# Scaling the token rows before the transpose, in place of a product with a diagonal, at three layer entrances

## The chip, the cores and the metric

The kernel runs on one core of one Trainium2 chip. The metric is the device time of one execution, in microseconds. Engines are named as in the profile: PE is TensorE (PEld its weight loads), DVE is VectorE, ACT is ScalarE, POOL is GpSimd, SP the engine that issues the weight DMAs.

## The reference, cut to what matters

Four mixers and two MLPs are applied in turn to 256 tokens of width 1024, all in f32. Each of them starts from a root-mean-square norm:

```python
def rms_norm(x, g):
    xf = x.astype(jnp.float32)
    y = xf * lax.rsqrt(jnp.mean(xf * xf, axis=-1, keepdims=True) + NORM_EPS)
    return (y * g.astype(jnp.float32)).astype(x.dtype)

def adaln_pre_norm(x, c, g, w_mod, b_mod):
    mod = jax.nn.silu(c) @ w_mod + b_mod
    shift, scale, gate = jnp.split(mod, 3, axis=-1)
    h = rms_norm_2(x, g, NORM_EPS) * (1.0 + scale[:, None, :]) + shift[:, None, :]
    return h, gate
```

The order is: sparse attention (dsa), MLP 0, the RWKV mixer, MLP 1, a norm in the middle, a short convolution mixer (conv), a dilated attention mixer (dil), a last norm. The three entrances of this case are those of the RWKV mixer (plain `rms_norm`), of conv and of dil (both `adaln_pre_norm`).

## The kernel before, in words

The activations `X` lie with the tokens on the partitions, as two tiles of 128 tokens by 1024. Each linear layer wants them with the features on the partitions, in eight blocks of 128. Weights come as granules of 128x1024 into a ring of four slots: SP's DMA fills `raw`, ACT rounds it to `w_hi` (L737), DVE takes the rest `w_lo` (L1350, `split_lo`), and PE makes three products per tile (hi·hi, hi·lo, lo·hi). The activations are split in the same way into `act_hi` (ACT) and `act_lo` (DVE). Each engine has its own program, written out by hand in a fixed order, and semaphores join them. SP may load granule g once `w_lo` of granule g-4 is made, and ACT may round it once PE is done with granule g-4.

An entrance goes as follows, for token tile i = 0 and then 1. ACT sums the squares of `X` (L755). DVE adds the two partial sums and the epsilon (`total_sum`, L1364; at conv, where the middle norm comes in between, `mid_totals`, L1369 to L1374). POOL raises the sum to the power of minus one half (L561). DVE multiplies the identity with that root into a diagonal `diag`, which lies in the buffer `per_head` (`spread_rstd`, L1359). PE multiplies each of the tile's eight blocks with the diagonal (`turn_scaled`, L2390), which transposes the block and scales its tokens in one step. The results lie in four PSUM banks, two feature blocks in each; when tile 1's part of a bank is there, the semaphore `turned` is raised, and the bank's reader takes it: at the RWKV mixer ACT copies it to `hT` (L1038), and DVE then makes the differences `xx` (L1803) and the mixes (L1775); at conv and dil DVE scales it into `act_f` (`scale_turned`, L1385), ACT rounds it (L768) and DVE takes the rest (L1392). PE's first granules behind the entrance (`entering_features`, L2325) wait for these.

Beside the turns PE has small work there. `mod_columns` (L2724) sums the modulation's columns in eight one-column products, `mod_gate` (L2730) the gate rows, `fill` (L2712) makes products that nobody reads. At the RWKV mixer the first `mod_columns` stood between the turns of tile 0 and tile 1.

DVE has other work in the same stretch, in its fixed order: `add_down` (L1714) adds the MLP's last products to `X`, `gain_mid` (L1718) multiplies the middle norm's gain into `xn`, `split_lo` makes the next layer's first `w_lo`. Behind the conv entrance DVE still has the last `weigh_mod` (L1666) and two scalings of `X` (L2097) before the `w_lo` of conv's granule 4.

`mlp_turn` (L2401) is a turn without a scale: it uses `pe.transpose` on `X` with the identity, eight of them in a call.

## Time and profile before

| | us |
|---|---|
| time, median of 3 runs | 1066.27 |
| time, lowest and highest | 1065.84, 1067.09 |
| the profiled execution, span from first to last instruction | 1066.7 |
| PE busy | 1048.1 (98%) |
| PEld busy | 996.2 (93%) |
| DVE busy | 771.7 (72%) |
| ACT busy | 590.3 (55%) |
| POOL busy | 120.4 (11%) |

For the profiled execution the span is the only time that is recorded; it lies between the lowest and the highest of the timed runs. PE's busy time counts from each product's start to its modelled end, and the products overlap, so how fast PE works is read from the distance between starts. The granted clock of the core was 0.998 of full speed over the span. A product of two f32 operands appears as two records in the trace, a `pe.transpose` as one.

### The profile page before, as it was taken

The numbers are of one execution on the slowest core, as the hardware profiler recorded it, in microseconds if no ns is written. First come the engines' busy times: TensorE is split into PE (matmuls) and PEld (weight loads), VectorE is DVE, ScalarE is ACT, GpSimd is POOL, SyncE is SP. The second block draws the span as 40 slices with busy tenths as digits, with TensorE's granted clock in tenths as the row PEclk, the third lists the DMA queues.
The fourth block names the chain that finished last, engine by engine and source line by source line (L and its number), as shares of the span: only waits on it lengthen the run. The fifth ranks groups of instructions, "written<-read, shape, count | busy, mean of one in ns | idle before, by whom it ended". The sixth has DMA issues, their size and how long they took to land.

```text
span 1066.7 us, 25458 instructions
## 1 busy us (share of the span) xinstructions
PE 1048.1 (98%) x10480; PEld 996.2 (93%) x10485; DVE 771.7 (72%) x1090; ACT 590.3 (55%) x900; POOL 120.4 (11%) x131
## 2 busy tenths in 40 slices
PE   9999999999999999999999999999999999999997
PEld 8966999999999899997899999999998999999985
DVE  5987666766789689768766676786676877775586
ACT  6586555555456783334555454564544667666452
POOL 0230010100000028841000000000000000000000
PEclk9999999999999999999999999999999999999999
DMA  8734687888634510002678777737653656556401
GB/s 308 251 90 137 216 286 266 271 296 280 204 122 155 163 61 5 3 11 74 217 250 287 255 252 264 276 121 228 197 192 112 212 181 199 171 195 196 143 2 59
DMA packets 83073, 192.23 MB, mean 180 GB/s; under 512 B 6000, under 2 KB 6912, under 8 KB 82992
## 3 DMA queue, kind: packets, MB, share of 16 engines
q1 hardware_dynamic: 74256, 159.93, 45.3%
q0 software_dynamic: 7584, 27.53, 7.8%
q10 hardware_dynamic: 1152, 3.59, 1.0%
q8 instruction: 63, 1.03, 0.4%
q14 instruction: 18, 0.15, 0.0%
HBM read 189.45 MB, written 1.05 MB: 179 GB/s over the span
## 4 chain that ended last, share of the span: by engine, by line
PE 88%; DVE 6%; issue 2%; ACT 2%; DMA 2%; POOL 0%; DVEq 0%; POOLq 0%; ACTq 0%
PE bank L2308 13%; PE bank L2310 13%; PE bank L2309 13%; PE bank L2659 5%; PE bank L2658 5%; PE bank L2660 5%; PE bank L2325 4%; PE bank L2345 4%; PE bank L2877 4%; PE bank L2275 2%; PE bank L2276 2%; PE bank L2277 2%; PE bank L2263 1%; PE bank L2265 1%; PE bank L2264 1%
## 5 line engine op out<-in xcount | busy, mean ns | idle before, releaser
L1350 DVE TENSOR_TENSOR w_lo<-raw,w_hi 128x1024 fp32r<-128x1024 f32 x295 | 357.8, 1223 | 199.2 <-ACT w_hi L737 198.7
L737 ACT ACTIVATE w_hi<-raw 128x1024 fp32r<-128x1024 f32 x295 | 310.3, 1059 | 291.4 <-PE bank L2310 150.4
L2308 PE MATMUL bank<-act_hi,w_hi 128*128 128x256 f32 x1200 | 334.0, 278 | 0.4 <-DVE w_lo L1350 0.3
L2309 PE MATMUL bank<-act_lo,w_hi 128*128 128x256 f32 x1200 | 332.9, 277 | 0.0
L2310 PE MATMUL bank<-act_hi,w_lo 128*128 128x256 f32 x1200 | 332.8, 277 | 0.0
L2308 PEld LDWEIGHTS bank<-act_hi,w_hi 128*128 128x128 f32 x1200 | 225.3, 188 | 1.7 <-DVE w_lo L1350 0.9
L2310 PEld LDWEIGHTS bank<-act_hi,w_lo 128*128 128x128 f32 x1200 | 225.3, 188 | 0.0
L2309 PEld LDWEIGHTS bank<-act_lo,w_hi 128*128 128x128 f32 x1200 | 225.0, 187 | 0.0
L2658 PE MATMUL bank<-w_hi,ff_hi 128*128 128x256 f32 x512 | 141.5, 276 | 0.0
L2659 PE MATMUL bank<-w_lo,ff_hi 128*128 128x256 f32 x512 | 141.5, 276 | 0.0
L2660 PE MATMUL bank<-w_hi,ff_lo 128*128 128x256 f32 x512 | 141.5, 276 | 0.0
L2658 PEld LDWEIGHTS bank<-w_hi,ff_hi 128*128 128x128 f32 x512 | 96.1, 188 | 0.0
L2660 PEld LDWEIGHTS bank<-w_hi,ff_lo 128*128 128x128 f32 x512 | 96.1, 188 | 0.0
L2659 PEld LDWEIGHTS bank<-w_lo,ff_hi 128*128 128x128 f32 x512 | 96.1, 188 | 0.0
L590 POOL DMA_DIRECT2D mod_w<-in_w_mod_dram x48 | 25.8, 538 | 319.2 <-DVE mod_all L1666 239.2
L2275 PE MATMUL bank<-w_hi,act_hi 128*128 128x256 f32 x192 | 54.2, 282 | 0.0
L2276 PE MATMUL bank<-w_lo,act_hi 128*128 128x256 f32 x192 | 53.8, 280 | 0.0
L2277 PE MATMUL bank<-w_hi,act_lo 128*128 128x256 f32 x192 | 53.8, 280 | 0.0
L1666 DVE SCALAR_TENSOR_TENSOR mod_all<-mod_w,c_col,mod_all 128x1024 f32<-128x1024 f32 x42 | 52.5, 1278 | 0.0
L561 POOL TENSOR_TENSOR stat<-stat,half_neg 128x1 f32<-128x1 f32 x10 | 5.5, 553 | 405.9 <-DVE stat L1364 372.6
L2275 PEld LDWEIGHTS bank<-w_hi,act_hi 128*128 128x128 f32 x192 | 36.7, 191 | 1.0 <-issue 1.0
L2276 PEld LDWEIGHTS bank<-w_lo,act_hi 128*128 128x128 f32 x192 | 36.0, 188 | 0.0
(375 smaller groups left out, 1675.4 us busy)
## 6 DMA issues: line engine op xcount, KB each, us to landing
raw<-in_mlp_w_up_dram SPq DMA_DIRECT2D x64, 512.0 KB, 3.7
raw<-in_mlp_w_down_dram SPq DMA_DIRECT2D x64, 512.0 KB, 6.1
raw<-in_dil_w_in_dram SPq DMA_DIRECT2D x64, 512.0 KB, 4.1
mod_w<-in_w_mod_dram POOLq DMA_DIRECT2D x48, 512.0 KB, 5.9
raw<-in_conv_w_in_dram SPq DMA_DIRECT2D x32, 512.0 KB, 4.5
raw<-in_rwkv_w_rkv_dram SPq DMA_DIRECT2D x24, 512.0 KB, 4.1
raw<-in_dsa_w_in_dram SPq DMA_DIRECT2D x12, 512.0 KB, 8.1
raw<-in_dsa_w_o_dram SPq DMA_DIRECT2D x8, 512.0 KB, 4.5
```

The source lines that it names most:

```text
L737: act.activation(w_hi[:, slot, :], raw[:, slot, :], ACT.Copy).then_inc(hi_ready, 1)
L1350: dve.tensor_tensor(w_lo[:, slot, :], raw[:, slot, :], w_hi[:, slot, :].bitcast(F32), ALU.subtract).then_inc(lo_ready, 1)
L1666: dve.scalar_tensor_tensor(total, part, c, total, ALU.mult, ALU.add).then_inc(mod_used[n], 1)
L2275: pe.matmul(to, x_hi, w_hi[:, slot, cols], start=q == part == 0, stop=False, skip_group_check=True)
L2276: pe.matmul(to, x_hi, w_lo[:, slot, cols], start=False, stop=False, skip_group_check=True)
L2277: mm = pe.matmul(to, x_lo, w_hi[:, slot, cols], start=False, stop=q == PER_BLOCK - 1 and kk == 1, skip_group_check=True)
L2308: pe.matmul(dst, w_hi[:, slot, at], hi[:, kt, :], start=begin, stop=False, skip_group_check=True)
L2309: pe.matmul(dst, w_hi[:, slot, at], lo[:, kt, :], start=False, stop=False, skip_group_check=True)
L2310: mm = pe.matmul(dst, w_lo[:, slot, at], hi[:, kt, :], start=False, stop=end, skip_group_check=True)
L2658: pe.matmul(dst, x_hi, w_hi[:, at_slot, at], start=first and q == 0 and h == 0, stop=False, skip_group_check=True)
L2659: pe.matmul(dst, x_hi, w_lo[:, at_slot, at], start=False, stop=False, skip_group_check=True)
L2660: mm = pe.matmul(dst, x_lo, w_hi[:, at_slot, at], start=False, stop=last and q == PER_BLOCK - 1, skip_group_check=True)
```

## The change

At the three entrances `spread_rstd` is replaced by `scale_tile`: DVE multiplies the token tile itself by its reciprocal root, in four pieces of 128x256, into a buffer of its own (`x_scaled` at the RWKV mixer, `v_dil` at conv and dil), and raises `x_scaled` after each piece. `turn_scaled` then uses `pe.transpose` with the identity, and waits per piece instead of per tile. The first `mod_columns` of the RWKV entrance is moved ahead of the turns. In `mlp` the call for tile 0 comes one step later in DVE's order, behind `add_down(1, 1)` and, at conv, behind `gain_mid(1, 1)`.

```diff
@@ vector engine
+            def scale_tile(n, i):
+
+                dve.wait_ge(rstd_ready, TILES * n + i + 1)
+                for b in range(4):
+                    at = slice(2 * P * b, 2 * P * (b + 1))
+                    dve.tensor_scalar(TURN_BY[n][:, i, at], TURN_FROM[n][:, i, at], rstd[:, i:i + 1], None, ALU.mult).then_inc(x_scaled, 1)
...
                     add_down(1, 1)
-                    spread_rstd(2, 0)
                     gain_mid(1, 1)
+                    scale_tile(2, 0)
                     mid_totals(1)
                 else:
                     total_sum(0, 7)
-                    spread_rstd(1, 0)
                     dve.wait_ge(granule_used, base + 8 * FF_STEPS)
                     add_down(1, 1)
+                    scale_tile(1, 0)
                     total_sum(1, 8)
-                spread_rstd(1 + l, 1)
+                scale_tile(1 + l, 1)
                 split_lo(STREAM[following], 0)
...
                 total_sum(0, 21)
-                spread_rstd(3, 0)
+                scale_tile(3, 0)
                 split_lo(STREAM["dil"], 0)
                 add_tile("conv_out", 1, 1, 0, C["tmp"])
                 total_sum(1, 22)
-                spread_rstd(3, 1)
+                scale_tile(3, 1)
@@ tensor engine
-                    pe.wait_ge(diag_ready, TILES * n + i + 1)
                     for b in range(4):
+                        pe.wait_ge(x_scaled, 8 * (n - 1) + 4 * i + b + 1)
                         for kk in range(2):
...
-                            mm = pe.matmul(dst, src[:, i, kt * P:(kt + 1) * P], diag[:, i, :], start=True, stop=True)
+                            mm = pe.transpose(dst, TURN_BY[n][:, i, kt * P:(kt + 1) * P], ident)
...
-                turn_scaled(1, X, RKV_TURN, lambda: mod_columns(0, 0))
+                mod_columns(0, 0)
+                turn_scaled(1, RKV_TURN)
```

In the orders below the changed kernel's own line numbers stand, 16 higher from DVE's program on for the same line: its `scale_tile` is L1375, its turns are L2406. DVE's order at the end of MLP 1, where the conv entrance begins, was this before (`stat` holds the sums and roots):

```order
L1714 SCALAR_TENSOR_TENSOR X<-bank,stat,X 128x512
L1359 TENSOR_SCALAR per_head<-const,stat 128x128
L1718 TENSOR_TENSOR xn<-X,scale_row 128x512
L1369 TENSOR_SCALAR stat<-stat 128x1
L1371 TENSOR_SCALAR stat<-stat 128x1
L1374 TENSOR_TENSOR stat<-stat 128x1
L1359 TENSOR_SCALAR per_head<-const,stat 128x128
L1350 TENSOR_TENSOR w_lo<-raw,w_hi 128x1024
L1385 TENSOR_SCALAR act_f<-bank,gain,mod_col 128x256 x4
```

In the changed kernel the same place reads:

```order
L1730 SCALAR_TENSOR_TENSOR X<-bank,stat,X 128x512
L1734 TENSOR_TENSOR xn<-X,scale_row 128x512
L1375 TENSOR_SCALAR v_dil<-xn,stat 128x256 x4
L1385 TENSOR_SCALAR stat<-stat 128x1
L1387 TENSOR_SCALAR stat<-stat 128x1
L1390 TENSOR_TENSOR stat<-stat 128x1
L1375 TENSOR_SCALAR v_dil<-xn,stat 128x256 x4
L1359 TENSOR_TENSOR w_lo<-raw,w_hi 128x1024
L1401 TENSOR_SCALAR act_f<-bank,gain,mod_col 128x256 x4
```

The diagonal of tile 0 stood ahead of the last `gain_mid`; the four scalings now stand behind it and ahead of the sums of tile 1, and the four of tile 1 ahead of `w_lo`.

PE's order at the entrance of the RWKV mixer, behind the last products of MLP 0, was this before (`const` is the table with the identity and the ones):

```order
L2659 MATMUL bank<-w_lo,ff_hi 128x256
L2660 MATMUL bank<-w_hi,ff_lo 128x256
L2390 MATMUL bank<-per_head,X 128x128 x8
L2724 MATMUL bank<-const,mod_all 128x1 x8
L2390 MATMUL bank<-per_head,X 128x128 x8
L2724 MATMUL bank<-const,mod_all 128x1 x8
L2730 MATMUL bank<-mod_all,const 128x512 x2
```

In the changed kernel:

```order
L2675 MATMUL bank<-w_lo,ff_hi 128x256
L2676 MATMUL bank<-w_hi,ff_lo 128x256
L2740 MATMUL bank<-const,mod_all 128x1 x8
L2406 MATMUL bank<-const,x_scaled 128x128 x16
L2740 MATMUL bank<-const,mod_all 128x1 x8
L2746 MATMUL bank<-mod_all,const 128x512 x2
```

The first eight column products now stand ahead of all sixteen turns, and the turns read the scaled rows and the constant table.

DVE's order at the same entrance was this before:

```order
L1714 SCALAR_TENSOR_TENSOR X<-bank,stat,X 128x512 x3
L1364 TENSOR_SCALAR stat<-stat 128x1
L1359 TENSOR_SCALAR per_head<-const,stat 128x128
L1714 SCALAR_TENSOR_TENSOR X<-bank,stat,X 128x512
L1364 TENSOR_SCALAR stat<-stat 128x1
L1359 TENSOR_SCALAR per_head<-const,stat 128x128
L1350 TENSOR_TENSOR w_lo<-raw,w_hi 128x1024
L1803 TENSOR_TENSOR xx<-hT 128x512
```

In the changed kernel:

```order
L1730 SCALAR_TENSOR_TENSOR X<-bank,stat,X 128x512 x3
L1380 TENSOR_SCALAR stat<-stat 128x1
L1730 SCALAR_TENSOR_TENSOR X<-bank,stat,X 128x512
L1375 TENSOR_SCALAR x_scaled<-X,stat 128x256 x4
L1380 TENSOR_SCALAR stat<-stat 128x1
L1375 TENSOR_SCALAR x_scaled<-X,stat 128x256 x4
L1359 TENSOR_TENSOR w_lo<-raw,w_hi 128x1024
L1819 TENSOR_TENSOR xx<-hT 128x512
```

The scaling of tile 0 moved behind `add_down(1, 1)` and ahead of the sum of tile 1.

## Rows read from the trace of the kernel before

**Rows 1.** The page: busy times of the engines, and shares of the chain that ended last.

```profile
PE 1048.1 (98%) x10480; PEld 996.2 (93%) x10485; DVE 771.7 (72%) x1090; ACT 590.3 (55%) x900; POOL 120.4 (11%) x131
...
PE 88%; DVE 6%; issue 2%; ACT 2%; DMA 2%; POOL 0%; DVEq 0%; POOLq 0%; ACTq 0%
```

**Rows 2.** PEld timeline, plain transposes: start us, us, instruction, count.

```profile
525.69 0.90 PEld L2401 LDWEIGHTS bank<-const,X 128*128 128x128 f32 x8
526.55 1.01 PEld L2325 LDWEIGHTS bank<-act_hi,w_hi 128*128 128x128 f32 x8
```

**Rows 3.** PEld, then PE timeline at the entrance of the RWKV mixer.

```profile
293.54 1.86 PEld L2390 LDWEIGHTS bank<-per_head,X 128*128 128x128 f32 x16 [0.30 <-DVE per_head L1359]
295.32 1.87 PEld L2724 LDWEIGHTS bank<-const,mod_all 128*128 128x128 f32 x16
...
298.89 1.20 PEld L2724 LDWEIGHTS bank<-const,mod_all 128*128 128x128 f32 x10
...
302.39 1.22 PE L2325 MATMUL bank<-act_hi,w_hi 128*128 128x256 f32 x8
```

**Rows 4.** DVE groups by line and shape: count, busy us, mean ns, idle before.

```profile
L1385 DVE TENSOR_SCALAR act_f<-bank,gain,mod_col 128x256 f32<-128x256 f32 x16 | 7.7, 534 | 0.9 <-PE bank L2390 0.9
...
L2123 DVE TENSOR_SCALAR cv<-tpad,pcol 128x256 f32<-128x256 f32 x8 | 2.3, 347 | 0.0
...
L2097 DVE TENSOR_SCALAR X<-xn,stat 128x1024 f32<-128x1024 f32 x2 | 1.4, 750 | 0.0
```

**Rows 5.** DVE timeline within conv, the convolution's first taps.

```profile
742.38 1.14 DVE L2123 TENSOR_SCALAR cv<-tpad,pcol 128x256 f32<-128x256 f32 x4
```

**Rows 6.** DVE timeline at the entrance of the RWKV mixer.

```profile
293.48 0.75 DVE L1714 SCALAR_TENSOR_TENSOR X<-bank,stat,X 128x512 f32<-128x512 f32 x1
295.02 0.21 DVE L1364 TENSOR_SCALAR stat<-stat 128x1 f32<-128x1 f32 x1 [0.79 <-ACT xn L755]
295.90 0.29 DVE L1359 TENSOR_SCALAR per_head<-const,stat 128x128 f32<-128x128 f32 x1 [0.66 <-POOL stat L561]
...
298.87 0.69 DVE L1803 TENSOR_TENSOR xx<-hT 128x512 f32<-128x512 f32 x1 [1.55 <-ACT hT L1038]
...
302.13 0.16 DVE L1749 TENSOR_TENSOR mod_col<-bank,pcol 128x16 f32<-128x16 f32 x1
```

**Rows 7.** ACT timeline at the entrance of the RWKV mixer.

```profile
297.92 0.84 ACT L1038 ACTIVATE hT<-bank,pcol 128x256 f32<-128x256 f32 x2 [2.94 <-PE bank L2390]
```

**Rows 8.** DVE timeline at the conv entrance.

```profile
701.48 0.21 DVE L1369 TENSOR_SCALAR stat<-stat 128x1 f32<-128x1 f32 x1 [0.51 <-ACT act_f L755]
...
702.09 0.16 DVE L1374 TENSOR_TENSOR stat<-stat 128x1 f32<-128x1 f32 x1 [0.15 <-ACT act_lo L755]
702.91 0.29 DVE L1359 TENSOR_SCALAR per_head<-const,stat 128x128 f32<-128x128 f32 x1 [0.67 <-POOL stat L561]
703.12 1.22 DVE L1350 TENSOR_TENSOR w_lo<-raw,w_hi 128x1024 fp32r<-128x1024 f32 x1
704.38 1.90 DVE L1385 TENSOR_SCALAR act_f<-bank,gain,mod_col 128x256 f32<-128x256 f32 x4
...
716.62 4.63 DVE L1350 TENSOR_TENSOR w_lo<-raw,w_hi 128x1024 fp32r<-128x1024 f32 x4
```

**Rows 9.** ACT timeline at the conv entrance.

```profile
705.41 0.63 ACT L768 ACTIVATE act_hi<-act_f 128x512 fp32r<-128x512 f32 x1 [3.35 <-DVE act_f L1385]
```

**Rows 10.** PE timeline, first products of conv's granule 0 and of its granule 4.

```profile
707.15 1.04 PE L2325 MATMUL bank<-act_hi,w_hi 128*128 128x256 f32 x7
...
718.12 0.28 PE L2308 MATMUL bank<-act_hi,w_hi 128*128 128x256 f32 x1
```

**Rows 11.** DVE, then PE timeline at the dil entrance.

```profile
819.95 0.29 DVE L1359 TENSOR_SCALAR per_head<-const,stat 128x128 f32<-128x128 f32 x1 [0.66 <-POOL stat L561]
821.12 1.90 DVE L1385 TENSOR_SCALAR act_f<-bank,gain,mod_col 128x256 f32<-128x256 f32 x4 [0.88 <-PE bank L2390]
...
822.92 1.18 PE L2325 MATMUL bank<-act_hi,w_hi 128*128 128x256 f32 x8 [0.57 <-ACT act_hi L768]
```

More of the change, by code:

```diff
@@ L237, in program, with scaled_plan @@
         xn = scope(xn_plan)
+        def scaled_plan(t):
+            t("x_scaled_under", [P, 4 * KT * SEQ])
+            return t("x_scaled", [P, TILES, D])
+        scaled_x = scope(scaled_plan)
         def mixer_plan(t):
@@ L321, in program @@
         LA = scope(dil_att_plan)
+        TURN_FROM = {1: X, 2: xn, 3: X}
+        TURN_BY = {1: scaled_x, 2: L["v"], 3: L["v"]}
         def column(first, n=KT):
@@ L349, in program @@
         squared, rstd_ready, rstd_step = sem("squared"), sem("rstd_ready"), sem("rstd_step")
+        x_scaled = sem("x_scaled_by_rstd")
         diag_ready, sums_full, mid_total, mid_rooted = sem("diag_ready"), sem("sums_full"), sem("mid_total"), sem("mid_rooted")
@@ L2376, in turn_heads, with turn_scaled @@
                 mm.then_inc(turned, 1)
-            def turn_scaled(n, src, banks, between=None, ordered=False):
+            def turn_scaled(n, banks, between=None, ordered=False):
                 for i in range(TILES):
@@ L3078, in conv @@
                 mod_columns(1, 0)
-                turn_scaled(2, xn, LATE_TURN)
+                turn_scaled(2, LATE_TURN)
                 mod_columns(1, 1)
@@ L3106, in gates @@
                     mod_gate(1)
-                turn_scaled(3, X, LATE_TURN, gates, ordered=True)
+                turn_scaled(3, LATE_TURN, gates, ordered=True)
                 def begin_gates():
```

## The prediction

> **What bounds the kernel now.** I read the page first: PE is busy for 98% of the span and the chain that ended last lies on PE for 88% of it [rows 1]. So in general a microsecond taken from PE is a microsecond gained. Then I read the timelines of PE, DVE and ACT at each of the three entrances, since the change moves work from PE to DVE just there, and asked of each entrance what PE's next granule waits for.
>
> At the RWKV entrance it is DVE. PE is through with its gate products about when the features begin at 302.39, and these had to wait for DVE's `mod_col` at 302.13 [rows 3, 6]. That instruction hangs on an unbroken DVE sequence that began with `xx` at 298.87, and DVE had idled 1.55 us before it, waiting for ACT's first `hT` [rows 6], which in turn had waited 2.94 us for PE's first turned bank [rows 7]. At conv it is PE: DVE's first scaling started at 704.38, ACT's rounding at 705.41 was over at 706.04, and PE arrived at 707.15 [rows 8 to 10]. At dil it is the chain again: DVE waited 0.88 us for the turned bank, started at 821.12, and PE idled 0.57 us for ACT until 822.92 [rows 11].
>
> **What PE is spared.** With the diagonal, eight products of a tile took 295.32 - 293.54 = 1.78 us [rows 3]. Eight plain transposes took 526.55 - 525.69 = 0.86 us [rows 2], 0.107 us each: they appear as one record where an f32 product is two. The saving is 0.92 us a tile, six tiles, 5.5 us in all. This is the largest gain that is to be had, and only if nothing else then holds PE.
>
> The Trainium skill, in "TensorE: Matmul & The Clock Gate", Part 4 (PE-mode transpose), speaks against this: it gives about 275 ns for a 128x128 transpose within a kernel. Taken as the time that each one occupies PE, eight would be 2.2 us, more than the 1.78 us of now, and the sum further down would be some 0.5 us higher. The trace has starts 0.107 us apart, so I go by the trace.
>
> **What DVE is charged.** The trace has the same operation at the same shape, f32 128x256 from SBUF by a column: 347 ns [rows 4], four in 1.14 us [rows 5]. So the distance of two is (1.14 - 0.347)/3 = 0.264 us, and a tile takes 4 x 0.264 = 1.06 us of DVE's sequence; its first piece is there after 0.35 us, its last after 1.14. The diagonal took 0.21 (the next instruction started 703.12 - 702.91 later [rows 8]). The charge is 0.85 us a tile. The upper bound is the same shape from PSUM, 534 ns [rows 4], which with the same overlap of 0.08 us is 0.45 apart and 1.81 a tile; the pieces read SBUF, so I take 0.264.
>
> A single instruction over the tile took 750 ns [rows 4], so that cutting it into four costs about 0.4 us a tile. The Trainium skill says why it should: "VectorE: DVE Perf Modes", in the section on the TRN2 errata, has a fixed latency paid by each instruction and advises tiles of 512 or more. With its measured fixed term of 150 cycles a piece would be an estimated 290 ns, 0.1 us a tile more than my value, and the sum some 0.4 us higher.
>
> **RWKV entrance.** The scaling of tile 0 follows `add_down` (293.48, and 0.66 until the next can start [rows 6]): 294.14 to 295.20. Behind it is queued tile 1's sum, which could start at 295.02 [rows 6] and now starts at 295.20. From sum to scaling POOL takes 0.88 us, as before [rows 6], so tile 1 is scaled from 296.08 on (before: the diagonal at 295.90), first piece at 296.43, DVE free at 297.14. Next is `w_lo`, which is 1.14 long in sequence ((4.63 - 1.22)/3 [rows 8]): DVE is free for `xx` at 298.28.
>
> PE now starts `mod_columns` right behind MLP 0 at about 293.3; it is 1.79 us long (298.89 - 295.32 is one of it and one set of turns, 3.57 [rows 3]): 295.1. Tile 0's pieces are there, so 0.86 us of turns, 295.9, and then PE waits for tile 1's piece at 296.43. The first bank needs two transposes behind it, against four records behind 297.11 before, from which ACT started at 297.92, 0.81 later, 0.37 behind the last of them [rows 3, 7]. Now: 296.43 + 0.04 + 0.21 + 0.37 = 297.05, and with 0.84 [rows 7] `hT` is there at 297.89. That is ahead of 298.28, so `xx` starts at 298.32, not 298.87: **0.55 us earlier**. PE's rest (turns until 297.5, then `mod_columns` and gates, at most 302.39 - 298.89 = 3.50 [rows 3]) ends by 301.0, ahead of `mod_col` at 301.58. PE idles for DVE, but everything behind comes 0.55 us earlier. The same DVE sequence feeds PE until granule 4.
>
> **Conv entrance.** DVE was through with `gain_mid` at 700.97, since it idled 0.51 us ahead of tile 1's sum at 701.48 [rows 8]. `gain_mid` can move up by no more than 0.1 us when the diagonal ahead of it is gone, since it needs the result of `add_down`. So the scaling of tile 0 runs from about 700.81 to 701.87, and behind it are queued the three instructions of tile 1's sum. The third came 702.09 - 701.48 = 0.61 behind the first, 0.15 of it waiting for ACT [rows 8]; ACT is through by then, so it comes at 701.87 + 0.46 = 702.33, 0.24 us late. POOL takes the same 702.91 - 702.09 = 0.82 [rows 8]: scaling of tile 1 from 703.15 to 704.21, `w_lo` to 705.35, and only then the first `act_f`, against 704.38 [rows 8]: 0.97 us late.
>
> PE is early here: it needs 0.86 a tile, idles for tile 1's first piece at 703.50, and would be at the features at about 706.4. But behind `act_f` at 705.35 there are 1.03 us until ACT's rounding (705.41 - 704.38 [rows 8, 9]), 0.63 for it [rows 9] and 0.15 until PE (822.92 - 821.12 = 1.80 at dil holds the same three [rows 11]): 707.15, as now [rows 10]. All 1.8 us that PE is spared here become waiting.
>
> And DVE stays late. Between 704.38 and 716.62 I find no gap in its sequence, so `w_lo` of granule 4 moves from 716.62 to 717.59 and is there 1.22 us later, at 718.81 [rows 8]. PE took granule 4 up at 718.12, only 0.28 us behind 717.84, when its `w_lo` was there [rows 8, 10]. With 0.05 from DVE to PE it now takes it up at 718.86: **0.74 us later**. Behind it DVE makes a `w_lo` in 1.14 us where PE needs (718.12 - 707.15)/4 = 2.74 for a granule [rows 8, 10], so it stays at this one loss. SP's load of granule 8, behind the same `w_lo`, has four granules of room.
>
> **Dil entrance.** Nothing is charged ahead of tile 1: tile 0's scaling lies in the wait for PE's last conv products. Tile 1: scaling from 819.95, where the diagonal stood [rows 11], first piece at 820.30, first bank readable at 820.30 + 0.04 + 0.21 + 0.37 = 820.92, but DVE is in its own scaling until 821.01. `act_f` starts at 821.03, against 821.12: **0.09 us earlier**, and PE with it.
>
> **The sum.** -0.55 + 0.74 - 0.09 = +0.10 us. The profiled span is 1066.7, and with it 1066.8; it lies 0.4 above the median of 1066.27, and from there the forecast is **1066.4**. What a measurement of this kernel can tell from no change is about 0.2%, 2.1 us. This is far inside: no change.
>
> **Rivals.**
> - PE's saving carries through. Then up to 5.5 us are gained: 1060.8. For it: the 98% and 88% of rows 1. Against it: at all three entrances the rows show the next granule fed by DVE and ACT. To pass the bound of 2.1 us, conv would have to give back its 1.8 and lose nothing. 7 in 100.
> - Conv loses nothing, since DVE's sequence between 704.38 and 716.62 has gaps in which it catches up 0.8 us. Then -0.64: 1065.6. Against it: the first `act_f` started 0.12 behind the moment at which DVE could be through with `w_lo` (704.38 - 703.12 - 1.14 [rows 8]), and I find no larger gap. 13 in 100.
> - It is slower: DVE's pieces cost the PSUM distance of 0.45, because each raises a semaphore or because of where the buffer lies. A tile is then 0.75 us longer, and it counts twice at RWKV and conv (both tiles lie in the chain) and once at dil: +0.10 + 5 x 0.75 = +3.85, 1070.1. It passes the bound from (2.1 - 0.1)/5 = 0.4 us a tile, pieces 0.36 apart. Against it: the row of the taps. 9 in 100.
> - Transposes occupy PE for the 275 ns of the page named above. From rows: eight then take 2.2 us in place of 0.86. At conv the turns began 2 x 1.78 + 1.79 ahead of 707.15, at 701.8; 16 of 0.275 and the columns end at 708.0, 0.85 late, which contains granule 4's wait; dil loses an estimated 0.3, and RWKV keeps its 0.5, since DVE is slower there than PE. +0.6: 1066.9. 4 in 100.
> - The forecast: 67 in 100, by itself 1065.5 to 1067.4 (each of the three shifts may be off by some 0.3, and the runs of before span 1.25).
>
> **How the numbers follow.** Faster by over 0.2% is the first rival, 0.07. Slower is the third, 0.09. The rest is 0.84. The range leaves these two out, which are 16 in 100, and takes in the second and fourth with the runs' own spread: 1064.9 to 1067.8.
>
> **What the profile after would show.** Turns on PE: eight records in about 0.86 us for a tile; a wait on PE for DVE ahead of tile 1 of 0.5 us at RWKV and 0.75 us at conv. Scalings 0.26 apart. `xx` some 0.5 us sooner behind the end of MLP 0; `act_f` at conv 1.0 us later behind the end of MLP 1, PE idle about 0.8 us ahead of the features and again 0.7 us ahead of granule 4. Total PE busy down by some 5 us with the span unchanged. The forecast is wrong if the pieces are over 0.36 apart, if granule 4 is not late, or if some later stage, which I take to move as a whole, takes up or gives back more than the 0.1 us.

## The result, and the profile after

The changed kernel took 1074.14 us in the median of 4 runs (1071.19 to 1076.99), the kernel before 1066.05 in 4 (1062.18 to 1067.09), its three from ahead of the prediction among them. The ratio is 1.0097 with a 95% interval of 1.0067 to 1.0128: slower by about 1%, and outside the range given. Run again later it was 1074.38 (1073.57 to 1077.03, 4 runs), ratio 1.0116 [1.0087, 1.0145].

The span and clock, and then the line of busy times on the page of the changed kernel, which answers to [rows 1]:

```profile
core 0: 1070.0 us, clock 0.995
```

```profile
PE 1049.7 (98%) x10437; PEld 996.5 (93%) x10437; DVE 776.9 (73%) x1108; ACT 590.7 (55%) x900; POOL 121.1 (11%) x131
```

The clock is the granted TensorE clock over the span, as a share of full speed: 0.995, and 0.998 before. DVE's busy time is up by 5.2 us, six tiles at some 0.85, as was reckoned. PE's should have fallen by 5 and is up by 1.6.

PE timeline of the changed kernel at the RWKV entrance ([rows 3]) and at the conv entrance ([rows 10]):

```profile
294.37 1.07 PE L2406 MATMUL bank<-const,x_scaled 128*128 128x128 f32 x8
295.86 1.23 PE L2406 MATMUL bank<-const,x_scaled 128*128 128x128 f32 x8 [0.42 <-DVE x_scaled L1375]
...
301.17 1.18 PE L2341 MATMUL bank<-act_hi,w_hi 128*128 128x256 f32 x8 [0.57 <-issue]
...
702.09 1.23 PE L2406 MATMUL bank<-const,v_dil 128*128 128x128 f32 x8 [0.81 <-DVE v_dil L1375]
703.15 1.84 PE L2740 MATMUL bank<-const,mod_all 128*128 128x1 f32 x16
705.67 1.18 PE L2341 MATMUL bank<-act_hi,w_hi 128*128 128x256 f32 x8 [0.68 <-ACT act_hi L777]
706.69 1.70 PE L2341 MATMUL bank<-act_lo,w_hi 128*128 128x256 f32 x8
708.18 1.91 PE L2341 MATMUL bank<-act_hi,w_lo 128*128 128x256 f32 x8
709.89 1.31 PE L2341 MATMUL bank<-act_hi,w_hi 128*128 128x256 f32 x8
711.04 1.10 PE L2341 MATMUL bank<-act_lo,w_hi 128*128 128x256 f32 x8
711.98 1.10 PE L2341 MATMUL bank<-act_hi,w_lo 128*128 128x256 f32 x8
...
718.58 0.28 PE L2324 MATMUL bank<-act_hi,w_hi 128*128 128x256 f32 x1
```

DVE's timeline of the changed kernel at the same places ([rows 6, 8]):

```profile
292.87 0.75 DVE L1730 SCALAR_TENSOR_TENSOR X<-bank,stat,X 128x512 f32<-128x512 f32 x1 [0.96 <-PE bank L2676]
293.53 1.13 DVE L1375 TENSOR_SCALAR x_scaled<-X,stat 128x256 f32<-128x256 f32 x4
...
297.64 0.68 DVE L1819 TENSOR_TENSOR xx<-hT 128x512 f32<-128x512 f32 x1
...
703.87 1.90 DVE L1401 TENSOR_SCALAR act_f<-bank,gain,mod_col 128x256 f32<-128x256 f32 x4
...
716.11 3.49 DVE L1359 TENSOR_TENSOR w_lo<-raw,w_hi 128x1024 fp32r<-128x1024 f32 x3
```

Two things stand out on PE at conv. Eight products took 1.70 and 1.91 us where they otherwise take 1.10: that is the clock. And once it is back, the next group of eight starts 711.98 - 711.04 = 0.94 later, which over longer stretches is 0.1178 us from one product to the next. Here is the same place in the kernel before:

```profile
709.96 1.07 PE L2325 MATMUL bank<-act_hi,w_hi 128*128 128x256 f32 x8
710.87 1.07 PE L2325 MATMUL bank<-act_lo,w_hi 128*128 128x256 f32 x8
```

The groups start 710.87 - 709.96 = 0.91 apart; over longer stretches it is 0.1133 us a product, at the same granted clock. I call this distance the pace, 0.113 the fast one and 0.118 the slow one. The windows show clock and pace over longer stretches, first of the changed kernel, then of the kernel before and of only_dil (below). Behind the length stand the busy time and, in brackets, the count of instructions for PE, PEld, DVE, ACT and POOL, then the granted clock and DMA's share and GB/s:

```profile
706.00:708.00 2.00, 2.00 (x16) 2.00 (x15) 2.00 (x3) 1.94 (x3) 0.00 (x0) 0.73 0.49 186
708.00:710.00 2.00, 2.00 (x11) 2.00 (x11) 2.00 (x4) 0.63 (x1) 0.00 (x0) 0.50 0.60 151
...
830.00:960.00 130.00, 130.00 (x1106) 130.00 (x1105) 100.43 (x119) 87.07 (x113) 0.00 (x0) 1.00 0.59 189
```

```profile
706.00:708.00 2.00, 2.00 (x19) 2.00 (x19) 2.00 (x4) 2.00 (x4) 0.00 (x0) 1.00 0.63 229
...
830.00:960.00 130.00, 130.00 (x1106) 130.00 (x1106) 99.87 (x117) 86.78 (x113) 0.00 (x0) 1.00 0.60 191
```

```profile
830.00:960.00 130.00, 130.00 (x1149) 130.00 (x1148) 103.25 (x121) 90.56 (x120) 0.00 (x0) 1.00 0.62 197
```

Over 708 to 710 the changed kernel has clock 0.50, which is 1.2 of 2.4 GHz, and 11 products in 2 us. In these 130 us of dil both count 1106 products, the slow pace (at the fast one it is 1149; the last line is only_dil's, the change at dil alone). PE is busy all the time at either pace, so the column of busy time says nothing. At conv a count says little too, since the window also cuts into stages with other products. The time from the start of conv's first feature product to the start of what follows its 768 does: 87.13 us in the kernel before, 92.05 in the changed one.

**Where the 3.3 us between the two profiles lie.** I compare ACT's `w_hi` of the same granule and the starts above. At the end of MLP 0 the changed kernel is already 0.61 ahead, for no reason in the change. The RWKV entrance gives 0.62, RWKV and MLP 1 behind it 0.36: 1.59 ahead. At conv the features are 0.11 late against that, and the 768 products take 92.05 - 87.13 = 4.92 longer. Profiles with the slow pace and no fall of the clock there (before_filled, ident_seamless) have 90.64, so the pace costs 90.64 - 87.13 = 3.51 and the fall of the clock 1.41. (Granules 0 to 3 alone tell the same: 718.58 - 705.67 = 12.91 here, 11.49 in before_filled.) Together that makes the 5.05 by which the shift grows until the end of conv, +3.46. A second stretch at half clock behind the dil entrance takes it to +4.87; PE has eight transposes and waits of 0.90 and 1.22 us ahead of it. From 965 on the changed kernel is at the fast pace and the one before still at the slow one, which gives back 1.58: +3.29.

**Why the medians are further apart.** The 137 runs of the kernel before beside the experiments lie in two groups with few between: on one chip 19 of 35 at 1061.8 in the mean and 16 at 1069.0, on another 31 of 34 at 1062.1. The clock is 0.996 to 0.999 in both. I put the groups down to the pace of dil: its 1490 products in a row take 175.95 us in the profile before and 169.45 in that of wait_repeated, a kernel with the same work (below), 6.5 us less, and the two spans are 1066.7 and 1058.6. Each kernel has only one profile, so that the pace of dil differs between executions of one kernel is inferred from the groups. The profile before is from the upper group: most runs take 1.6 to 1.9 us more than their span, so its span of 1066.7 answers to some 1068.5 (the changed kernel's of 1070.0 has 1071.86), and its dil is at 0.118. All 8 runs of the changed kernel lie at 1071 and above.

### The profile page after: what moved, and what is told of

It is laid out like the page before. It is cut to its first block, busy times and chain, and to the rows that moved or that the text cites. A ratio compares the mean times of both kernels' runs of the same rounds, so it can differ in the third digit from the quotient of the medians.

```text
span 1070.0 us, 25385 instructions
## 1 busy us (share of the span) xinstructions
PE 1049.7 (98%) x10437; PEld 996.5 (93%) x10437; DVE 776.9 (73%) x1108; ACT 590.7 (55%) x900; POOL 121.1 (11%) x131
## 4 chain that ended last, share of the span: by engine, by line
PE 88%; DVE 6%; ACT 2%; issue 2%; DMA 2%; POOL 0%; SPq 0%; DVEq 0%; POOLq 0%; ACTq 0%
PE bank L2326 13%; PE bank L2324 13%; PE bank L2325 13%; PE bank L2341 6%; PE bank L2674 5%; PE bank L2676 5%; PE bank L2675 5%; PE bank L2361 4%; PE bank L2894 4%; PE bank L2291 2%; PE bank L2292 2%; PE bank L2293 2%; PE bank L2279 1%; PE bank L2281 1%; PE bank L2280 1%
## 5 line engine op out<-in xcount | busy, mean ns | idle before, releaser
L2325 PE MATMUL bank<-act_lo,w_hi 128*128 128x256 f32 x1200 | 333.6, 278 | 0.0
L2325 PEld LDWEIGHTS bank<-act_lo,w_hi 128*128 128x128 f32 x1200 | 225.5, 188 | 0.0
```

The lines of the kernel that those rows point to most:

```text
L2325: pe.matmul(dst, w_hi[:, slot, at], lo[:, kt, :], start=False, stop=False, skip_group_check=True)
```

## The experiments

All ratios are to the kernel before, run beside it on the same chip, with their 95% interval. They aren't the quotients of the medians: with two groups 7 us apart a median jumps from one to the other, so where it matters I compare the groups on one chip. "Pace" is the distance of 256-column products at full clock in the kernel's one profile. Fillers are the kernel's own `fill`: products that nobody reads. No kernel leaves out work. The line numbers of PE's features (L2325, L2341, L2342, L2345) differ from kernel to kernel for the same line.

**One entrance at a time.** The change at one entrance and the diagonal at the other two; of DVE's calls one each is shown, PE's follow them. The fourth kernel has the whole change and fillers at conv, and at dil two in the middle of the turns and three ahead of the features:

```diff
 only_rkv
-                scale_tile(3, 0)
+                spread_rstd(3, 0)
 only_conv
-                    scale_tile(1, 0)
+                    spread_rstd(1, 0)
 after_filled: the whole change, and
-                turn_scaled(2, LATE_TURN)
+                turn_scaled(2, LATE_TURN, lambda: fill(2, 1))
                 mod_columns(1, 1)
+                fill(2, 1)
```

> The change at the RWKV entrance alone. Theory W (the loss comes from PE's new waits: behind a wait PE's products follow each other 118 ns apart instead of 113, and the clock falls to 1.2 GHz for 3.4 us where the waits lie among one-column products and transposes): this entrance gains its 0.6 us, since PE's pace behind it was 118 before too; 0.6 us below before, unless the clock falls there. Theory D (the loss is the 0.86 us a tile of DVE's work): the same -0.6 us. Theory T (pe.transpose by itself lowers the clock, waits or not): some 1.7 us above before.

> The change at the conv entrance alone. Theory W: +0.8 to 1.1 us for DVE's lateness, +3.5 us for 768 products of conv at 118 instead of 113 ns, and 1.2 to 1.7 us where the clock falls: 5 to 6.5 us above before. Theory D: +0.8 to +1.1 us and PE's pace in conv stays at 113. Theory T: +1.7 us for the clock, and pace 113.

> The change at the dil entrance alone. Theory W: -0.1 us at the entrance and +1.7 us if the clock falls behind it as in the changed kernel; the pace of dil was 118 before already, so no more: 0 to 2 us above before. Theory D: -0.1 us. Theory T: as W.

> The changed kernel, with products that nobody reads in place of PE's waits: two of 128x256 f32 (0.43 us each) ahead of tile 1's turns and two ahead of the features at conv, two and three of them at dil. Theory W: the clock stays at 2.4 GHz and conv goes at 113 ns, so that the time comes back to between 1.5 us below and 1 us above before (dil may even take the faster pace, some 7 us below). Theory D: stays above before by what it is now, since DVE's work is the same. Theory T: stays too, since all transposes are there.

| 12 runs each | median us | ratio | pace conv, dil |
|---|---|---|---|
| only_rkv | 1066.93 | 0.9989 [0.9959, 1.0019] | 0.113, 0.118 |
| only_conv | 1071.30 | 1.0032 [1.0006, 1.0059] | 0.118, 0.118 |
| only_dil | 1067.59 | 1.0014 [0.9989, 1.0039] | 0.113, 0.113 |
| after_filled | 1071.35 | 1.0045 [1.0011, 1.0078] | 0.118, 0.118 |

Only the conv entrance alone has a loss clear of the noise. The parts don't add up to the whole (0.32% and 0.14% less 0.11%, against 0.97% and 1.16%): the whole was measured in other rounds, and chips and rounds differ in how often the kernel before is in its upper group. The RWKV entrance alone costs nothing: its four lower runs average 1060.05 and its eight upper 1067.42, where those of the kernel before on this chip have 1061.78 and 1068.99, 1.7 and 1.6 more, but the interval holds 1. The fillers took most falls of the clock away (0.996 or more in 9 of 12 runs, against 0.988 to 0.995 in all 8 of the changed kernel) and left conv's pace at 0.118 in the profile. Not in every run, it seems: one run took 1060.53 and another 1063.87, 3.3 apart. With conv at the slow pace the lower group of only_rkv, 1060.05, would come to an estimated 1063.6; so the first of the two hardly had it.

**A wait alone.** The kernel before, with PE waiting ahead of conv's features for ACT's second rounding, and the same place with a wait that is already met:

```diff
 before_wait
                 mod_columns(1, 1)
+                pe.wait_ge(act_hi_ready, 4 * 4 + 2)
 wait_repeated
                 mod_columns(1, 1)
+                pe.wait_ge(act_hi_ready, 4 * 4 + 1)
```

> The kernel before with one wait more: ahead of conv's first features PE waits until ACT has rounded the second pair of feature blocks too, about 0.4 us. No work is changed. Theory P (a wait of PE ahead of a long row of products draws its pace anew, 113 or 118 ns apart, and keeps it; before has one such draw, at dil, which is why its runs lie in two groups about 7 us apart): runs in up to four groups, as conv and dil draw each, about 3.5 and 7 us apart: the lowest near 1062, others near 1065.5, 1069 and 1072.5, the median at least 1.5 us above before. Rival D (a wait costs its own length): both groups of before, each 0.4 us or less higher.

> The kernel before, with the wait that conv's first features have anyway (ACT's first rounding) written once more ahead of it: no time is added, one instruction of PE's queue is. Theory Q (the pace hangs on how the instructions lie in PE's queue): conv at 118 ns, both groups of before about 3.5 us higher. Theory P (it is the time of waiting that spoils the pace): no change, groups near 1061.8 and 1068.8 as before.

before_wait: 1072.08, 1.0076 [1.0056, 1.0097]. PE timeline:

```profile
704.46 1.84 PE L2747 MATMUL bank<-const,mod_all 128*128 128x1 f32 x16
706.57 2.01 PE L2342 MATMUL bank<-act_hi,w_hi 128*128 128x256 f32 x8 [0.27 <-ACT act_hi L778]
708.38 1.88 PE L2342 MATMUL bank<-act_lo,w_hi 128*128 128x256 f32 x8
710.09 1.11 PE L2342 MATMUL bank<-act_hi,w_lo 128*128 128x256 f32 x8
711.03 1.10 PE L2342 MATMUL bank<-act_hi,w_hi 128*128 128x256 f32 x8
711.98 1.10 PE L2342 MATMUL bank<-act_lo,w_hi 128*128 128x256 f32 x8
```

The wait is 0.27 us long, and behind it stand both: products at half clock, and then 0.118 for all of conv. There is no scaled tile and no transpose at this entrance. wait_repeated: 1061.40, 1.0007 [0.9986, 1.0027], pace 0.113 at conv and dil, as if nothing was there:

```profile
706.69 1.07 PE L2342 MATMUL bank<-act_lo,w_hi 128*128 128x256 f32 x8
707.59 1.07 PE L2342 MATMUL bank<-act_hi,w_lo 128*128 128x256 f32 x8
```

So it is waiting that costs, and not an instruction more. By ratio (1.0076, against 1.0097 and 1.0116) it makes up most of the loss of the changed kernel. The groups say how: three runs of before_wait average 1065.7, 3.6 above the lower group on this chip (1062.1), which is conv's pace; the other eight average 1072.6 and have dil at the slow pace as well, by their level. The kernel before had 3 of 34 runs in its upper group there. So the wait at conv goes together with a slow dil more often too, and by an estimate from these counts that is the larger part of the ratio: (8/11 - 3/34) x 7 = 4.5 us, beside the 3.6. Nothing here shows why. The clock is 0.996 to 0.999 in the 11 runs, as before; its share is small.

**Products in place of transposes.** The changed kernel with a plain f32 product by the identity, which occupies PE as long as the product by the diagonal did:

```diff
-                            mm = pe.transpose(dst, TURN_BY[n][:, i, kt * P:(kt + 1) * P], ident)
+                            mm = pe.matmul(dst, TURN_BY[n][:, i, kt * P:(kt + 1) * P], ident, start=True, stop=True)
```

> The changed kernel, with the plain product of the scaled rows with the identity (two records, 1.78 us a tile) in place of pe.transpose. PE is slower by 0.92 us a tile and so has hardly a wait at conv. Theory P with the clock: no fall of the clock at conv (0.997 or more unless dil has one), less often the pace of 118 there; 1 to 5 us below the changed kernel, near 1063 to 1071. Rival D: the same DVE work, so the same time as the changed kernel or later.

1065.45, 1.0040 [1.0020, 1.0060]: 7 of 11 runs at 1065.2 and 4 at 1071.4 in the mean, the clock 0.997 or 0.998 in all. Its PE timeline:

```profile
704.82 1.84 PE L2740 MATMUL bank<-const,mod_all 128*128 128x1 f32 x16
706.52 1.19 PE L2341 MATMUL bank<-act_hi,w_hi 128*128 128x256 f32 x8
707.55 1.10 PE L2341 MATMUL bank<-act_lo,w_hi 128*128 128x256 f32 x8
...
718.32 0.36 PE L2324 MATMUL bank<-act_hi,w_hi 128*128 128x256 f32 x1 [0.25 <-DVE w_lo L1359]
```

With the time that the transposes save handed back to PE, there is no fall of the clock. A wait for granule 4's `w_lo` is there, of 0.25 us, as the prediction's sum has it but shorter, since PE is slower. The lower runs lie 3.1 above those of the kernel before on this chip (1062.1), conv's pace. Yet no wait stands ahead of the features here; only ahead of tile 1's turns one weight load starts 0.12 us late. So this run gives the clock back and not the pace.

**Fillers and columns.** The wait ahead of the features closed by fillers, at conv in only_conv (conv_full), at dil in only_rkv (dil_filled), or by one-column products of the constant table (dil_columns, after_columns; `columns`):

```diff
 conv_full
-                turn_scaled(2, LATE_TURN)
+                turn_scaled(2, LATE_TURN, lambda: fill(2, 1))
                 mod_columns(1, 1)
+                fill(4, 1)
 dil_filled
                 turn_scaled(3, LATE_TURN, gates, ordered=True)
+                fill(2, 1)
 dil_columns
                 turn_scaled(3, LATE_TURN, gates, ordered=True)
+                columns(5, 1)
```

> The change at conv alone, and products that nobody reads (two ahead of tile 1's turns, four ahead of the features, 0.43 us each) so that PE is never without work there and comes to granule 4 behind DVE's late w_lo. Theory P with the clock: no draw at conv, clock 0.997 or more, so that all of conv goes at 113 ns: two groups as before has them, each 1.0 to 1.6 us higher (the fillers' surplus), near 1063 and 1070. Rival D (DVE's work and the transposes are the loss): as the change at conv alone, 1065.5 to 1074.

> The change at the RWKV entrance alone, and two products that nobody reads (0.86 us) ahead of dil's features in place of the 0.57 us for which PE waits there in the kernel before. Theory P: PE goes from conv into dil without a wait and keeps 113 ns; nearly all runs in the lower group, near 1061.5, and the median 1 to 7 us below before. Rival D: both groups of the RWKV change alone (1060 and 1067.5), each 0.3 us higher.

> The changed kernel, nothing of it undone, with PE kept at work: two f32 products of 128x256 in place of the wait ahead of tile 1's turns at conv and at dil, and ahead of the features nine one-column products (0.22 us each) at conv and nine at dil, which nobody reads. The same kind stands directly ahead of conv's features in the kernel before. Theory P (PE's pace is settled at the first products of the features: 113 ns when one-column products run straight into them and what they wait for is long there, else a draw or 118; and the clock falls only in the thin stretches with waits): conv and dil both at 113 ns, clock 0.997 or more, 1061 to 1064 us in most runs, 6 to 12 us below the changed kernel on the same chip. Rival D (DVE's scalings and the order are the loss): the fillers can't help, 1070 or more.

> The change at the RWKV entrance alone, and five one-column products (1.1 us) ahead of dil's features, so that PE doesn't wait there. Theory P: dil at 113 ns in all runs: one group near 1061, none at 1067. Rival (any product ahead of the features gives 118, as the f32 fillers did): one group near 1067.

> The changed kernel itself, again, on the chip of the others. All theories: 5 to 12 us above the lower group of before (1061.8). Theory P: groups that go with the paces of conv and dil and the clock, the lowest near 1066, most between 1069 and 1077; with a profile in which conv or dil stands at 118 ns.

| | median us, runs | ratio | pace conv, dil |
|---|---|---|---|
| conv_full | 1066.79, 11 | 1.0050 [1.0029, 1.0070] | 0.118, 0.113 |
| dil_filled | 1066.92, 11 | 1.0044 [1.0030, 1.0059] | 0.113, 0.118 |
| dil_columns | 1067.92, 7 | 1.0056 [1.0036, 1.0076] | 0.113, 0.118 |
| after_columns | 1075.95, 5 | 1.0111 [1.0083, 1.0138] | 0.118, 0.118 |
| after_again | 1074.38, 4 | 1.0116 [1.0087, 1.0145] | 0.118, 0.118 |

The expectation that fillers bring the pace back was wrong. At dil they even seem to take it away: none of the 18 runs of dil_filled and dil_columns is in a lower group (the lowest is 1066.04), where the kernel before had 31 of 34 and 9 of 11 there. In after_columns, with more one-column products and no wait at conv, the clock falls at conv all the same: 0.989 in its profile.

**DVE's order.** To close the wait ahead of the features without a filler, DVE's first `w_lo`, the last `weigh_mod` and two scalings of `X` were put later, with the change at RWKV and conv and two fillers ahead of tile 1's turns (reordered), and with none of it and no filler (reordered_none); the cut shows the `w_lo` alone:

```diff
-                split_lo(STREAM[following], 0)
+                if l == 0:
+                    split_lo(STREAM[following], 0)
...
+                split_lo(base, 0)
                 scale_turned(5, 1, act_f, gain[:, 0, :], f_ready, mod_col[:, 0, 0:KT], LATE_TURN)
```

> The change at the RWKV and conv entrances, dil as before. DVE's order at conv is changed: the first w_lo of conv stands behind the first act_f, and the last weighing of the modulation and the two scalings of X stand behind the w_lo of granule 7 instead of ahead of granule 4. Two f32 products stand in place of the wait ahead of tile 1's turns. So PE comes to the features, and to granule 4, behind what they need. Theory P: conv at 113 ns, groups as before's, at its level or up to 1.5 us below: near 1061 and 1068. Theory Q: no forecast of the pace; with 118, near 1064.5 and 1071.5.

> The kernel before with DVE's new order at conv alone (as in the run with both entrances, but with the diagonals). PE didn't wait there and doesn't now: both theories expect no change, groups near 1061.8 and 1068.8.

1070.47, 1.0088 [1.0061, 1.0115], and 1070.53, 1.0083 [1.0054, 1.0112]. Both missed. The order makes `act_lo` late: in reordered PE waits 0.37 us for it inside granule 0. In reordered_none there is hardly a wait to be seen:

```profile
707.62 1.16 PE L2345 MATMUL bank<-act_hi,w_hi 128*128 128x256 f32 x8
708.61 1.13 PE L2345 MATMUL bank<-act_lo,w_hi 128*128 128x256 f32 x8
709.58 1.10 PE L2345 MATMUL bank<-act_hi,w_lo 128*128 128x256 f32 x8
```

The first eight have the fast pace (708.61 - 707.62 = 0.99; before, 1.00), the second group has one start late by 0.03 us, when `act_lo` came, and everything behind it is at 0.118. The clock stays at 0.999. This shows the slow pace by itself, without a fall of the clock; that the late start brought it is read from where it begins, and no run tests it.

**Gaps closed, and fillers alone.** Is it any gap at the entrance, or the changed turns?

```diff
 after_seamless: the changed kernel; ident_seamless: ident with fill(1) and fill(2); ident_end: ident_seamless without the first
-                turn_scaled(2, LATE_TURN)
+                turn_scaled(2, LATE_TURN, lambda: fill(3, 1))
                 mod_columns(1, 1)
+                fill(3, 1)
 before_filled: the kernel before
                 mod_columns(1, 1)
+                fill(2, 1)
```

> The changed kernel with three products that nobody reads ahead of tile 1's turns at conv and three ahead of the features. Measured so far: in all ten profiles in which the weight loads at the conv entrance had any gap of 0.03 us or more, wherever it lay, conv's products came 0.118 us apart; in the six without one, 0.113. In the filled kernel a gap of 0.10 us was left ahead of tile 1's turns, four of 0.05 among them and 0.21 ahead of granule 4. Here none should be left. Theory A (any gap in PE's queue between MLP 1 and conv's granule 4 sets the pace of conv, the transposes themselves do not): conv at 0.113 in the profile, about 3.5 us less than the filled kernel from the features to the end of conv, no fall of the clock at conv; the runs in two groups by dil's pace, near 1061.5 and 1068.5. Rival B (the scaled buffer, the transposes or the products in place set the pace, the gap does not matter): conv stays at 0.118, groups near 1065 and 1072.

> The changed kernel with plain products by the identity in place of the transposes, one product that nobody reads ahead of tile 1's turns at conv and two ahead of the features. With the plain products alone a gap of 0.12 us was left ahead of tile 1's turns, and one of 0.25 ahead of granule 4. Theory A (any gap sets the pace): no gap, conv at 0.113, runs in two groups near 1062 and 1069. Rival B (the gap does not matter): conv at 0.118, groups near 1065.5 and 1072.5.

> As the kernel ident_seamless, without the one product ahead of tile 1's turns, so that the gap of 0.12 us stays there and the one ahead of granule 4 is gone. Theory A (any gap sets the pace): conv at 0.118 from its first products, groups near 1065.5 and 1072.5, some 3.5 us above ident_seamless, from one product less. Rival B: the same pace and time as ident_seamless. Rival C (only a gap inside the stage counts): conv at 0.113, as ident_seamless.

> The kernel before, with two products that nobody reads ahead of conv's features and nothing else; PE waits for nothing there, as before. The kernels with their gaps closed by such fillers kept conv at 0.118 us. Theory A2 (a gap in PE's queue costs the pace, and a filling product directly ahead of the features costs it too, so that a filler cannot give it back): conv at 0.118 in the profile, runs in two groups near 1065.5 and 1072.5. Rival B2 (the filler does nothing to the pace, what costs it in the filled kernels is the changed turns): conv at 0.113, runs near 1062 and 1069, about 0.5 above the kernel before.

| | median us, runs | ratio | pace conv |
|---|---|---|---|
| after_seamless | 1069.73, 12 | 1.0038 [1.0009, 1.0067] | 0.118 |
| ident_seamless | 1066.75, 12 | 1.0038 [1.0012, 1.0065] | 0.118 |
| ident_end | 1073.13, 8 | 1.0075 [1.0049, 1.0102] | 0.118 |
| before_filled | 1072.24, 12 | 1.0047 [1.0019, 1.0074] | 0.118 |

In after_seamless and ident_seamless no gap was left, and the pace stayed at 0.118: theory A fell as it was put. ident_end kept ident's late weight load ahead of tile 1's turns. before_filled says why these three could not decide it. The kernel before with two fillers directly ahead of the features, no wait and no changed turn, loses the pace too:

```profile
709.50 1.11 PE L2735 MATMUL bank<-const 128*128 128x256 f32 x4
710.26 1.29 PE L2342 MATMUL bank<-act_hi,w_hi 128*128 128x256 f32 x8
711.39 1.10 PE L2342 MATMUL bank<-act_lo,w_hi 128*128 128x256 f32 x8
712.33 1.11 PE L2342 MATMUL bank<-act_hi,w_lo 128*128 128x256 f32 x8
```

Four of its runs average 1066.2 and eight 1072.7.

Over the 20 profiles: six have neither a late start of PE or of its weight loads (0.03 us or more) between the first turn and granule 0's end, nor a filler directly ahead of the features, and conv is at 0.113 in all six; fourteen have one or both, and conv is at 0.118 in all fourteen. In ident_seamless, after_seamless and before_filled it is the filler alone. That is a regularity of conv's profiles, not a mechanism. At dil it doesn't hold: behind the same wait of 0.57 us the pace is 0.118 in seven profiles and 0.113 in five, and behind one of 1.2 us 0.118 in three and 0.113 in one (only_dil). Nor does a change of pace need a wait: in MLP 0 of the kernel before, products start 0.118 apart until 140.5 us and 0.113 from there, where the down products begin, with no idle between. What in PE holds the pace stays open. So does, for ident, whether the gap of 0.12 us far ahead of the features does it: every kernel that closed it did so with a filler and lost the pace by that.

## Why the prediction was wrong

**The arithmetic of the entrances held.** Four scalings took 1.13 and 1.14 us, so pieces 0.26 apart, and not the 0.29 of the estimate beside that sum. `xx` came 297.64 - 292.87 = 4.77 behind the start of the last `add_down`, before 5.39 [rows 6]: 0.62 earlier for 0.55. At conv `w_lo` of granule 4 started at 716.11, which with the 1.59 that the kernel was ahead is 1.08 late against [rows 8], for 0.97. The features at conv are 0.11 late for 0, `act_f` at dil 0.11 early for 0.09. PE waited 0.42 us for tile 1 at RWKV (0.5 was named) and 0.81 at conv (0.75).

**Eight transposes** of a tile that was there started 0.109 us apart, for 0.107 from [rows 2]. Tile 1's went in pairs 0.26 apart, at the pace of DVE's pieces, so that its turns took 703.15 - 702.09 = 1.06 and not 0.86. The rows give one of them as 285 ns:

```profile
L2406 PE MATMUL bank<-const,v_dil 128*128 128x128 f32 x32 | 4.6, 285 | 1.7 <-DVE v_dil L1375 1.7
```

The Trainium skill's 275 ns ("TensorE: Matmul & The Clock Gate", Part 4, PE-mode transpose), given there for bf16, agrees with that as the time from start to end of one; as the time that one occupies PE the trace does not bear it out. The rival built on it was wrong, though PE lost time at the transposes in another way.

**The step that failed** is "All 1.8 us that PE is spared here become waiting", taken to cost nothing, and with it "some later stage, which I take to move as a whole". In the kernel before PE has no wait from 640 us, within MLP 1, to the dil entrance. The change put 0.81 us of waiting ahead of tile 1's turns and 0.68 ahead of the features (above). Waiting was priced at nothing. In the profile conv's 768 products then took 4.92 us longer than before, 3.51 by the pace and 1.41 by the clock, and a second fall of the clock behind the dil entrance cost about as much again. before_wait shows that such a wait is enough, with nothing else changed: 3.5 us for conv's pace, and in its profile a fall of the clock besides. ident shows the clock's part from the other side: take back what PE is spared, and the falls of the clock go. The pace doesn't come back in ident, so that the waits alone set it in the changed kernel is not shown.

**"... it stays at this one loss" of 0.74 at granule 4** did not come about. The `w_lo` was there at 716.11 + 1.22 = 717.33; PE at its old pace from 705.67 would have been there at 716.64 and waited 0.74, as predicted. With the clock down and the slow pace it came at 718.58. The lost time hid the wait: granule 4 is 2.05 late, not 0.74.

**The baseline** was mis-sized as well. The three runs that I had looked like one level with a spread of 1.25. They were three draws of which all fell, by their level, in the upper of two groups 7 us apart, which was chance; 96 of the 137 runs of the kernel before now lie in the lower one. "What a measurement of this kernel can tell from no change is about 0.2%" and the range of 1064.9 to 1067.8 were too narrow by that alone.

**The rivals.** PE's saving did not carry through and conv did lose; DVE's pieces were not at the PSUM distance. The slower side was given 0.09, all of it for DVE. That PE would pay for its own idleness was no case of mine.

Shown by runs: that a short wait ahead of conv's features is enough for the slow pace of conv and, by ratio, for most of the loss (before_wait against wait_repeated), and that the falls of the clock go when PE is not spared (ident). Argued from profiles and groups: that the pace of dil makes the two groups, and that it is slow more often behind a slow conv. Not shown: what sets conv's pace in the changed kernel beside the wait, and that its dil is always at 0.118. None of its 8 runs is below 1071, but its clock is down to 0.988 in some, and the time lost by that can hide a fast dil. Better than both kernels none is shown to be. only_rkv, with a highest run of 1068.07 against a lowest of 1071.19, beats the changed kernel; against the one before its interval holds 1.

## What to carry to other kernels

On the engine that bounds the kernel, work that is taken away ahead of a wait isn't time gained and may be time lost: look up whether that engine has any wait between there and the end of the next long stage, and if it has none, price the first one by a run before relying on zero. Compare paces by the distance of starts, or by the time of the same products in a row, since busy time hides them and a count in a window also depends on what else the window holds. And before a range is set from three runs, look in the trace for stages that can come out at either of two levels, and widen it by what they differ by, here 3.5 us for conv and 6.5 for dil.

## What the runs showed of the hardware

- f32 products of 256 columns start 0.1133 or 0.1178 us apart at the same granted clock of 1.00, and keep the one or the other for all 768 of conv (87.13 or 90.64 us) and for over 1100 of dil (1149 or 1106 in 130 us). The kernel before has both in one profile.
- In reordered_none one start at conv is 0.03 us late, and all starts behind it in the stage are 0.118 apart.
- At dil, behind the same wait of 0.57 us, profiles of different kernels have the one pace or the other (before 175.95 us for 1490 products, wait_repeated 169.45). The two groups of each kernel's runs suggest that it is drawn anew in each execution.
- The granted clock fell to 0.50 (1.2 GHz) at conv in six profiles. Ahead of it PE had been with one-column products (0.11 us from one record to the next) and, in five of them, waits of 0.17 to 0.81 us; before_wait has no transpose there and after_columns no wait. A fall at conv cost 1.4 us (after, after_again, before_wait) to 2.4 us (only_conv). The kernel before has the same one-column products with no wait, and no fall. With fillers in the waits the clock mostly stayed up (0.996 or more in 9 of 12 runs of after_filled and 10 of 12 of after_seamless).
